# Two-layer decoder trunk on one core: GpSimd's order of moves and loads at the end of a quad of heads, and the slots of the last four gates

## The reference, cut to what matters

```python
kv = shared_kv(x, kv_norm, w_kv)                 # K and V of three groups, 6 x 2048 columns
parts = split(rmsnorm(x, b_norm) @ b_w_in, 4)    # Q of three groups, and z
for g in groups: o_g, lse_g = dilated_branch(Q_g, K_g, V_g)   # scores + T5 bias, softmax, times V
o = sum_g softmax_g(lse) * o_g
y = o * silu(parts[-1])                          # the gate, made from z
x = x + y @ b_w_out
return rmsnorm(x, final_norm)
```

## Time and profile before

| | |
|---|---|
| median of 3 runs | 1419.02 us (1419.01 to 1427.1) |
| the profiled execution | 1420.43 us, its span 1418.6 us |
| granted clock of PE over the span | 0.993 of full |
| PE busy | 1394.5 us (98%) |
| DVE, ACT, POOL busy | 862.2, 698.3, 509.2 us |
| DMA | 315.64 MB, mean 222 GB/s |

### The profile page before, as it was taken

One profiled execution on the slowest core, in us unless ns is written; L12 is line 12 of the kernel. 1 busy time (PEld: TensorE's weight loads), 2 busy tenths in 40 slices (PEclk: granted clock), 3 DMA queues, 4 the chain that ended last, 5 costly groups with the idle time before them and its releaser, 6 DMA issues.

```text
span 1418.6 us, 19446 instructions
## 1 busy us (share of the span) xinstructions
PE 1394.5 (98%) x7444; PEld 1205.8 (85%) x7444; DVE 862.2 (61%) x1381; ACT 698.3 (49%) x1002; POOL 509.2 (36%) x445
## 2 busy tenths in 40 slices
PE   9999999999999999999999999999999999989997
PEld 8999999988888888888887888888788888868886
DVE  5999999632545545656654455666446655649642
ACT  5444444675644444545443445454445454436543
POOL 2988888888300010202203020220302202306474
PEclk9999999999999999999999999999999999999999
DMA  9866766655777779878778787877887879868851
GB/s 254 230 179 190 194 181 192 191 182 179 236 253 213 220 229 269 244 233 246 219 210 239 252 262 216 252 224 223 224 268 236 241 209 267 227 185 251 313 197 70
DMA packets 306093, 315.64 MB, mean 222 GB/s; under 512 B 76891, under 2 KB 196267, under 8 KB 305628
## 3 DMA queue, kind: packets, MB, share of 16 engines
q1 hardware_dynamic: 294268, 293.72, 68.9%
q0 software_dynamic: 11264, 19.94, 5.5%
q10 hardware_dynamic: 480, 0.90, 0.2%
HBM read 281.95 MB, written 24.71 MB: 216 GB/s over the span
## 4 chain that ended last, share of the span: by engine, by line
PE 86%; DMA 4%; DVE 4%; POOL 2%; issue 1%; ACT 1%; SPq 1%; DVEq 0%; POOLq 0%; ACTq 0%
PE bank L510 19%; PE bank L512 19%; PE bank L511 19%; PE bank L543 6%; PE bank L544 6%; PE bank L545 6%; PE bank L564 2%; PE bank L565 2%; PE bank L563 2%; POOL prob L627 2%; DMA kqz_dram<-sq_stage 2%; DVE w_lo L504 1%; DMA prob<-prob_sq 1%; PE bank L1743 1%; PE bank L1700 1%
## 5 line engine op out<-in xcount | busy, mean ns | idle before, releaser
L504 DVE TENSOR_TENSOR w_lo<-raw,w_hi 128x1024 fp32r<-128x1024 f32 x328 | 398.8, 1227 | 360.2 <-ACT w_hi L497 359.4
L497 ACT ACTIVATE w_hi<-raw 128x1024 fp32r<-128x1024 f32 x352 | 370.1, 1058 | 395.2 <-PE bank L512 390.6
L465 POOL TENSOR_TENSOR w_lo<-raw,w_hi 128x1024 fp32r<-128x1024 f32 x123 | 294.7, 2411 | 72.4 <-ACT w_hi L456 46.8
L510 PE MATMUL bank<-w_hi,mem_a 128*128 128x512 f32 x768 | 301.7, 393 | 6.1 <-DVE w_lo L504 6.1
L511 PE MATMUL bank<-w_lo,mem_a 128*128 128x512 f32 x768 | 301.0, 392 | 0.0
L512 PE MATMUL bank<-w_hi,mem_a 128*128 128x512 f32 x768 | 300.5, 391 | 0.0
L510 PE MATMUL bank<-w_hi,mem_b 128*128 128x512 f32 x640 | 249.4, 390 | 0.0
L511 PE MATMUL bank<-w_lo,mem_b 128*128 128x512 f32 x640 | 249.1, 389 | 0.0
L512 PE MATMUL bank<-w_hi,mem_b 128*128 128x512 f32 x640 | 249.0, 389 | 0.0
L543 PE MATMUL bank<-mem_a,w_hi 128*128 128x256 f32 x736 | 206.6, 281 | 0.7 <-DVE mem_a L1176 0.7
L544 PE MATMUL bank<-mem_a,w_hi 128*128 128x256 f32 x736 | 205.5, 279 | 0.0
(11 more groups left out here) (222 smaller groups left out, 1490.2 us busy)
## 6 DMA issues: line engine op xcount, KB each, us to landing
raw<-w_kv_dram SPq DMA_DIRECT2D x96, 1024.0 KB, 5.6
raw<-b_w_in_dram SPq DMA_DIRECT2D x64, 1024.0 KB, 5.7
raw<-a_w_in_dram SPq DMA_DIRECT2D x45, 1024.0 KB, 5.9
raw<-a_w_out_dram SPq DMA_DIRECT2D x16, 1024.0 KB, 5.3
raw<-b_w_out_dram SPq DMA_DIRECT2D x16, 1024.0 KB, 7.8
kqz_dram<-sq_stage SPq DMA_DIRECT2D x28, 512.0 KB, 7.3
prob<-prob_sq POOLq DMA_DIRECT2D x224, 32.0 KB, 4.8
kq_even<-kqz_dram POOLq DMA_DIRECT2D x32, 192.0 KB, 4.8
```

The costliest lines, as they stand in the source:

```text
L465: eng.tensor_tensor(w_lo[:, stream.half_slot(half), :], raw[:, slot, part:part + HALF], w_hi[:, stream.half_slot(half), :].bitcast(F32), A ...
L497: nc.scalar.activation(w_hi[:, w_slot(half), :], raw[:, s % RAW_SLABS, part:part + HALF], ACT.Copy).then_inc(hi_done, 1)
L504: eng.tensor_tensor(w_lo[:, w_slot(half), :], raw[:, s % RAW_SLABS, part:part + HALF], w_hi[:, w_slot(half), :].bitcast(F32), ALU.subtract ...
L510: nc.tensor.matmul(dst, operand(kt, 0, t), hi, start=(kt == 0), stop=False)
```

## The change

POOL issues the sixteen moves of the probabilities of a quad's last head ahead of the eight loads of K and Q for the next quad's first two heads. A function `gate_slot` gives the slot of `tanh_gate`: as before for heads 0 to 11, and 158, 160, 162, 164 for heads 12 to 15 (154, 157, 160, 162 before). DVE's `gate_head` stands one slot behind it for the first twelve heads, as before, and in the same slot for the last four (155, 158, 161, 163 before); it also moves out of the block of `normalise`.

```diff
+def gate_slot(h):
+
+    return SCORES_AFTER[h] + 4 if h < LATE else W_SLABS - 2 + 2 * (h - LATE)
...
                 move_squares(pool, first + 2, prob_turned)
+                move_squares(pool, first + 3, prob_turned)
                 load_kq(first + 4)
                 load_kq(first + 5)
-                move_squares(pool, first + 3, prob_turned)
...
-                    if s == SCORES_AFTER[h] + 4:
+                    if s == gate_slot(h):
                         tanh_gate(h)
...
+                    if s == gate_slot(h) + (h < LATE):
+                        gate_head(h)
                     if s == SCORES_AFTER[h] + 5:
-                        gate_head(h)
                         normalise(h)
```

## The result

| | before | changed |
|---|---|---|
| median | 1419.01 us (4 runs, 1416.09 to 1427.1) | 1398.70 us (4 runs, 1397.9 to 1399.1) |
| profiled execution, its span | 1420.43, 1418.6 | 1397.9, 1396.1 |
| granted clock over the span | 0.993 | 0.998 |
| PE idle from 380 us on | 13.8 us in five gaps | none |
| ACT, waits for moved probabilities | 33.5 us in three | none |

The ratio is 0.9847, with a 95% interval of 0.9807 to 0.9888: 1.5% faster, 20.3 us in the medians. The work is the same, 19446 instructions and 315.64 MB in both.

The account below looks back on a forecast made before the run. PE was taken as the bound, with its gaps and half clock to win: 12.6 us at three quad ends plus 8.0 in the last quad, 20.6 from the median 1419.02, gives 1398.4 us; range 1396.5 to 1406.5.

Parts of the forecast that it names:

- The sum of 20.6 us: PE's losses between heads' score matmuls: 6.25, 4.74 and 1.63 us at three quad ends, 5.42 and 2.54 in the last quad.
- Moves ready early, loads not delayed: POOL at quad ends: squares ready at 746.83, moves issued by 755.5, before the store ends at 756.69, so loads lose nothing.
- The wait that takes over: ACT at quad ends: waits 0 to 3.5 us for K and Q instead of 11.1 for moves; nothing reaches PE.
- rival C: Store, moves and raw loads share the DMA engines badly at quad ends; saving falls to about 9 us, 1410; chance 0.06.
- The margin of 7.8 us: ACT may be late by 7.8 us before PE notices: its wait of 11.08 became a PE gap of 3.3.
- A gap costs its idle time and the half clock: PE behind a gap runs at 1.2 GHz before 2.4 GHz; a gap of 3.3 us cost 6.25.
- Last quad, first part: Early moves bring z to about 1263, about 10 us earlier; most of the 5.42 and 2.54 us losses go.
- Last quad, second part: Four gates later: `tanh_gate(12)` to slot 158, its 13.0 us wait gone; tail stretch 0, bounds -0.4 to +0.4.
- What is next late: SP in the last quad: slab loads beside the z store and z loads; 0 to 4 us lost, taken as 0.
- rival B: Last quad keeps its loss: SP's chain becomes late, 8.0 us return, 1406.4; half of it, 1402.4; chance 0.12.
- D: Rival: POOL's order does nothing, squares released later than the store, z gate hidden by the next wait; 1419; chance 0.05.
- E: Rival, slower: K and Q behind all sixteen moves at `head_hi(4)`, slot 71, land at 776.0 or later; 1423 to 1431; chance 0.05.

Follow-up runs that it names:

- the first group of experiments: Four kernels on one chip beside the kernel before; the changed kernel, run again there, measured 1398.21 us, ratio 0.9826.
- The first part alone: Kernel before with only POOL's moves put ahead of the K and Q loads, the four gates in their old slots: 1399.98 us, ratio 0.9837.
- the gates alone: Changed kernel with POOL's order of before, so only the four gates of the last quad are late: 1415.98 us, ratio 0.9962.
- the run with thirty-two issues: Changed kernel with thirty-two idle DMAs on POOL between moves and K and Q loads at three quad ends: 1419.90 us, ratio 1.0001.
- sixteen issues: Changed kernel with sixteen idle DMAs on POOL between moves and K and Q loads at three quad ends: 1407.53 us, ratio 0.9924.

## Why the prediction was right, point by point

- **The time.** 1398.4 forecast, 1398.70 measured; 1399.8 for the profiled execution, which took 1397.9. That the medians meet within 0.3 us is luck in part: the kernel before scatters over 11 us in its four runs, and the same pair of kernels lies 22.2 us apart in the first group of experiments. What the 20.6 us rest on is the next point.
- **The sum of 20.6 us.** From the first score matmul of head 0 to that of head 15 the timelines differ by 20.7 us (728.19 before, 707.46 after). Here the prediction erred slightly: it took head 11's start from the chain of waits (1203.06) and head 12's from the timeline, in which head 11 starts at 1202.89, and so gave the third quad end 1.63 in place of 1.80. The further 1.8 us between the profiled executions lie outside this stretch, 0.85 ahead of it and 0.9 behind. Behind it PE's wait of 0.8 before the last `attend`, which the prediction let stand, is gone.
- **Moves ready early, loads not delayed.** As worked out: the moves are issued from 746.27, and against head 3's scores (729.94, in the timeline before 730.79) the loads start at 26.75 in place of 26.19, 0.6 us later. The store of the last Q chunk took 7.7 us beside the moves, between the 7.1 of before and the 8.3 that I took.
- **The wait that takes over.** I gave 0 to 3.5 us and took 0; it is 0.58 at the first end, up to 3.82 at the third, 7.4 in all. In the second profile of the same kernel it is 6.51 at the first end, where the store took 9.4 us and not 8.3 and the loads 7.4 and not 4.2. So the range was too short by 3 us, toward what rival C describes, and 1.3 us of the margin were left.
- **The margin of 7.8 us.** It was read off one gap and holds at all fourteen at the first two quad ends. The prediction used it for the third end and the last quad too. At the third end it is 10.3, which the rows of before gave already (a wait of 11.8 and a gap of 1.6), for `tanh_gate(12)` 7.7 (13.00 less 5.28), and for DVE's wait for the bias of head 13 it is 7.5.
- **A gap costs its idle time and the half clock.** True of twelve of the thirteen gaps from 2.69 to 5.28 us, which cost 1.6 to 3.1 us above their length. The thirteenth, of 3.17 us, left the clock at 1.00. So did those up to 1.6 us, and such gaps cost some 0.3 us above their length. Whether a gap near 3 us brings the half clock can't be told from its length alone.
- **The rule on the shared port.** The Trainium skill, SBUF — State Buffer, section SBUF: two separate sides, has GpSimd locked out while VectorE runs an operation in a 2-port perf mode. The prediction took that for whatever VectorE does there. Sixteen moves took 8.44 us in their new place, beside four `w_lo` of DVE, which are subtractions of two inputs, as 8.43 before, and 8.40 to 8.47 in every run. So no run here shows POOL's issues slowed by DVE. Whether an operation beside them was in the mode that the page means, no row shows.
- **Last quad, first part.** z a little past 1252 in the new time, that is 1263 less the 11.0 us saved ahead of it; its last load was issued by 1250.42, and such a load takes 1.9. The first part alone closes the gap between heads 12 and 14, as the text had it.
- **Last quad, second part.** Its worth beside the first I put at nothing on PE's path, with bounds of 0.4 either way in the tail. It is about 1.8 us in the medians, and 1.4 in the tail of the two profiles. Taken alone it is 4.5 us and not the 8.0 of the sum, because of the bias.
- **What is next late.** I named this chain (z store, z loads, slab loads, V store, bias) as rival B, with the right place and a chance of 0.12, but argued against it from three quads that show no loss. That argument was weak, since only the last quad has heads three slabs apart. What kept B away is that the first part draws the whole chain ahead: SP issues the bias 14.8 us behind head 12's scores in the changed kernel, 21.8 behind them with the gates alone. With K and Q only 6 us later, B is there. The forecast was nearer to it than I knew: in the changed kernel the bias of head 13 lands 0.2 us before DVE takes it (1252.61 + 9.7 against 1262.56), so that with the 7.5 of DVE some 7.7 us separate it from a gap. The prediction worked out the time of z in this chain and not that of the bias.
- **C, D and E** did not occur. E's point, K and Q near 776 us, is passed in the run with thirty-two issues (777.57): 1419.90, so all that was gained is lost.

## What to carry to other kernels

When a queue issues groups in a fixed order, look for the group whose data are ready while the one ahead of it still waits; swapping them costs nothing as long as the first fits into that wait. Price a gap by the distance between two marks of the bound engine and not by its idle rows, and find by how much the engine that feeds it may be late at that place. Here that was 7.8 us at two quad ends and 10.3 at the third, and it told which waits were free. When a wait near the end of a fixed queue is taken away, follow the queue on to the next small DMA that somebody needs, since its place counts as much as that of the big ones.

## What the runs showed that I had not expected

The kernel before scatters from 1415.82 to 1428.34 us over 17 executions of one group, the changed one from 1397.75 to 1398.92 over five on the same chip. The kernels that kept gaps scatter too (1404.41 to 1412.75 with sixteen issues), those without a gap stay within 1.6 us. The long executions have the lower mean granted clock: 1415.82 us at 0.996 and 1428.34 at 0.991, which by an estimate is 7 of the 12.5 us (0.005 of 1420). One part of the scatter is thus whether and for how long a gap brings the half clock, as at the gaps of 3.17 and 3.28 us above. The other I take to be the gap's length, since it hangs on when DMAs land, which varies, and a margin absorbs that; no run tests this by itself.
